# Another order for the front of a two-layer trunk: attention scores before v and u, modulation chunks under routing and residuals, ring slots by release

## The chip, the cores and the metric

The kernel runs on one core of one Trainium2 chip. The metric is device time in microseconds of one execution. Before the change three runs gave a median of 911.49 us (908.78 to 912.89).

## What is computed

`x` is 256 tokens by 1,024 channels, `c` one vector of 1,024; everything is float32. There are two layers. The reference, cut to what matters here:

```
cs = silu(c)
for i in range(2):
    sh_m, sc_m, g_m, sh_f, sc_f, g_f = split(cs @ w_mod[i] + b_mod[i], 6)     # 6 vectors of 1024
    h = rmsnorm(x) * (1 + sc_m) + sh_m
    y = hybrid_ab(h) if i == 0 else multiscale_pool(h)
    x = x + g_m * y
    h = rmsnorm(x) * (1 + sc_f) + sh_f
    x = x + g_f * hier_moe(h)      # 32 experts, 2 per token, chosen in 1 of 4 groups
hybrid_ab: q, kv_lat, q_idx, k_idx, w_idx, u, v = split(h @ w_in)
    A: indexer score picks 64 keys per query (top_k); 8 heads of 64 share one k, v
       made from rmsnorm(kv_lat) @ w_kv_up; softmax with a distance penalty; p @ v
    B: gelu(u) * (W_s @ layernorm(gelu(v)) + b_s), per chunk of 128 positions
    concat(A, B) @ w_o
```

## The kernel before

Each engine has a program of its own with its order written out by hand; semaphores (`S[...]`) join them. Nothing is reordered at run time, so on each engine a waiting instruction holds all that is queued behind it. TensorE's program is `_(pe)`, ScalarE's `_(act)`, VectorE's `_(dve)`, GpSimd's `_(pool)`; the loads of the large weights are issued by SyncE (`_(sp)`).

**The ring.** The tile `ring` has four slots of 2 MB. `plan` lists 31 chunks in the order in which TensorE uses them: 24 chunks `("mod", m)` (a modulation vector has two, m = 0 to 11 for layer 0 and 12 to 23 for layer 1), qi, kv, q, v and u of `w_in`, and two halves of `w_o`. Chunk n goes to slot n % 4 and is loaded once chunk n - 4 has been used (`chunk_done`). After the 21st chunk the expert loop of layer 0 takes over the ring: a pair of experts needs two slots for gate and up (4 MB) and the tile `dn_w` for down (2 MB); the last pair's down goes into the ring too. After that loop ten more chunks come, then the expert loop of layer 1. `FIRST` is the index of the first chunk after the first loop, `pair_slots` the two slots of a pair.

**Modulation.** `mod_chunk(m)` multiplies a chunk into four partial sums in a PSUM bank (line 424, 16 instructions); ScalarE copies them out (line 775, `mod_split`); `finish(m)` then sums them: a gate by two kinds of row matmul (lines 432 and 433), which ScalarE keeps in `gates` (line 779), or, after the second half of a shift or scale, a column of 8 values per partition by one-column matmuls (line 442, and 445 where the bias comes from `rows`; those are the "natural" ones of layer 1's mixer). The order is set by `mod_run(ms)`, on TensorE one chunk ahead of the finish, on ScalarE copy and keep chunk by chunk. `scale_shift` on VectorE waits for the columns (`col_kept`), and `modulated` makes `hT`, which all projections read.

**Layer 0's front.** On TensorE: mods 0 to 3, qi, kv, mods 4 and 5, indexer scores (`head_units`, line 522), `w_s` turned, q (line 482), v (543), mods 6 and 7, k and v of the attention (549, 551), u (482), mods 8 and 9, the spatial gating (563), attention scores (522), then turns of p (579) and p @ v (587), the output projection (610). VectorE selects the 64 keys meanwhile (lines 1096 to 1098), then does gelu and layernorm of v, gelu of u, `shift(u)` (penalty, mask, maximum; from line 1135) and `divide(u)` for six units of heads.

**Residual and routing.** `residual` adds the gated branch in four parts; ScalarE's `squares` and VectorE's `normed` follow, `turn` transposes (470). `route(l)`: router logits (624), the choice on VectorE with small count matmuls between (630 to 640), the selection matrix `sel` (1250), gathering of tokens (648), four rows turned (653). Then `experts(l)`: per pair gate and up (672), turn (682), down (694), combine (708). In `route(0)` TensorE runs mods 10 and 11 ahead of `turn` and mods 22 and 23 behind line 653; ScalarE has `squares` behind `mod_run(10, 11)`. Behind `experts(0)` come mods 12 to 15, `turn(2)`, mods 16 and 17, pooling (749), and in `route(1)` mods 18 to 21.

Of the kernel before, what the change touches and what calls it, by code (L numbers as in the profile page):

```python
# [37 lines left out]
def trunk(nc, x, c, w_mod, b_mod, norm_mix, norm_ffn, w_in, kv_norm, w_kv_up, sgu_norm, w_s, b_s, w_o,  # L38
# [19 lines left out]
    with ExitStack() as ctx:  # L58
# [48 lines left out]
        def chunk_at(n):  # L107
            s = (n % CH) * KT * HALF
            return ring[:, s:s + KT * HALF].rearrange("p (k n) -> p k n", k=KT)

# [13 lines left out]
        qiT, gtmp, qT, uT = ar(0, 1024, t=4), ar(1024, 1024, t=2), ar(2048, 1024, t=4), ar(3072, 1024, t=4)  # L124
# [6 lines left out]
        ws_raw, usq = ar(3072, 512, g=4), ar(0, 1024, t=4)  # L131
# [3 lines left out]
        att1 = hT[:, :, :].rearrange("p k t -> p (k t)").rearrange("p (h s) -> p h s", h=8)  # L135
# [19 lines left out]
        def v3(a, n):  # L155
# [15 lines left out]
        chunk_dmas = [2 if key == ("in", "kv") else 1 for key in plan]  # L171

        def arrivals(n):
            return 16 * sum(chunk_dmas[i] for i in range(n % CH, n + 1, CH))

        def mod_part(m):
            return dn_w[:, 1, 0, :] if 12 <= m < 22 else gates[:, 3, :]
# [17 lines left out]
            mix_done sgu_done bT_ready  # L195
# [15 lines left out]
        def pair_slots(l, b):  # L211

            first, second = ((FIRST, len(plan))[l] + 2 * b) % CH, ((FIRST, len(plan))[l] + 2 * b + 1) % CH
            return min(first, second), max(first, second)
# [12 lines left out]
        def _(sp):  # L227
# [5 lines left out]
            def chunk(n):  # L233

                kind, what = plan[n]
                dst, arrived = chunk_at(n), chunk_in[n % CH]
# [33 lines left out]
            for l in range(L):  # L270
# [3 lines left out]
                if l == 1:  # L274
                    sp.wait_ge(S["mix_done"], 10)
                    sp.wait_ge(S["col_kept"], len(columns))
# [16 lines left out]
                if l == 0:  # L293

                    first, second = pair_slots(l, 0)
# [104 lines left out]
        def _(pe):  # L400
            def arrived(key):

                n = chunk_no[key]
                pe.wait_ge(chunk_in[n % CH], arrivals(n))
# [6 lines left out]
            def mod_chunk(m):  # L411
# [8 lines left out]
                if m == 11:  # L420
                    pe.wait_ge(S["pT_ready"], 6)
# [79 lines left out]
            pe.wait_ge(S["small_in"], 16 * SMALL)  # L501
# [95 lines left out]
            for v in range(2, 6):  # L597
                turn_p(v)
# [810 lines left out]
```

## Time and profile before

| what | value |
|---|---|
| median of 3 runs | 911.49 us |
| the profiled execution | 918.24 us, span 916.5 us |
| TensorE busy, its weight loads | 780.9 us (85%), 387.7 us (42%) |
| VectorE, ScalarE, GpSimd busy | 241.9, 162.7, 36.8 us |
| moved | 269.59 MB, 294 GB/s over the span |
| mean granted TensorE clock | 0.891 of full |

### The profile page before, as it was taken

Reading aid. Unit: us, or ns where it says so; the run is one execution under the profiler, and the core shown is the slowest. Engines: PE = TensorE matmul, PEld = TensorE weight load, DVE = VectorE, ACT = ScalarE, POOL = GpSimd, SP = SyncE. Lnnn points to the kernel's source line nnn. Section 1 sums busy time; section 2 is a strip of 40 time slices with the busy share of each in tenths; the row PEclk is TensorE's granted clock in tenths of the full one; section 3 lists DMA queues with packets and bytes.
Section 4 is the critical chain, followed back from the end, with each engine's and each line's share of the span. In section 5 each row is a group of like instructions: output and inputs, shape, how many; then the busy total and the mean of one; then the engine's idle time right before and its main releaser. Section 6 shows DMA issues by size and latency. Waiting matters only on the chain.

```text
span 916.5 us, 9000 instructions
## 1 busy us (share of the span) xinstructions
PE 780.9 (85%) x3194; PEld 387.7 (42%) x3194; DVE 241.9 (26%) x667; ACT 162.7 (18%) x331; POOL 36.8 (4%) x63
## 2 busy tenths in 40 slices
PE   3689999689567989999999969965898999999994
PEld 1375767343462333333333327454533333333331
DVE  0013621811251221212122222524322121212123
ACT  2013021410212211212121102021212111212111
POOL 7200000000200000000000000002000000000000
PEclk9687998589568999999999987865899999999998
DMA  9949267105605999999999799556099999999961
GB/s 308 329 146 351 83 236 257 68 0 188 270 1 195 374 421 421 397 423 414 423 414 421 311 340 346 185 189 270 1 356 422 420 408 418 408 419 407 419 261 46
DMA packets 62138, 269.59 MB, mean 294 GB/s; under 512 B 3950, under 2 KB 6094, under 8 KB 37536
## 3 DMA queue, kind: packets, MB, share of 16 engines
q1 hardware_dynamic: 61152, 268.22, 74.3%
q0 software_dynamic: 960, 1.02, 0.5%
q8 instruction: 16, 0.26, 0.1%
q14 instruction: 10, 0.08, 0.0%
HBM read 268.18 MB, written 1.05 MB: 294 GB/s over the span
## 4 chain that ended last, share of the span: by engine, by line
PE 40%; issue 32%; DMA 18%; DVE 4%; ACT 3%; SPq 1%; POOL 1%; ACTq 0%; DVEq 0%; POOLq 0%
DMA ring<-in_w_up 13%; PE bank L672 7%; PE bank L482 5%; DMA ring<-in_w_mod 5%; PE bank L424 4%; PE bank L694 3%; PE bank L442 3%; PE bank L610 3%; PE bank L543 1%; PE bank L433 1%; PE bank L522 1%; PE bank L470 1%; PE bank L432 1%; PE bank L587 1%; PE bank L648 1%
## 5 line engine op out<-in xcount | busy, mean ns | idle before, releaser
L672 PE MATMUL bank<-ring,arena 128*64 128x512 f32 x1024 | 230.4, 602 | 31.4 <-DMA ring<-in_w_up 26.4
L672 PEld LDWEIGHTS bank<-ring,arena 128*64 128x64 f32 x1024 | 82.9, 138 | 158.6 <-issue 151.9
L708 PE MATMUL bank<-arena 128*128 128x512 f32 x256 | 117.9, 604 | 0.0
L694 PE MATMUL bank<-dn_w,hT 128*64 128x512 f32 x480 | 108.8, 592 | 0.6 <-DMA dn_w<-in_w_down 0.6
L1292 DVE SCALAR_TENSOR_TENSOR hT<-hT,bank 128x256 f32<-128x256 f32 x32 | 13.5, 421 | 238.0 <-ACT hT L935 238.0
L708 PEld LDWEIGHTS bank<-arena 128*128 128x128 f32 x256 | 46.2, 189 | 71.2 <-issue 71.2
L424 PE MATMUL bank<-ring,cs 128*32 128x512 f32 x384 | 53.6, 698 | 19.0 <-DMA ring<-in_w_mod 18.3
L694 PEld LDWEIGHTS bank<-dn_w,hT 128*64 128x64 f32 x480 | 40.0, 137 | 63.8 <-issue 61.8
L482 PE MATMUL bank<-hT,ring 128*128 128x256 f32 x192 | 47.4, 413 | 2.9 <-ACT hT L803 2.9
L935 ACT ACTIVATE hT<-bank 128x256 f32<-128x256 f32 x32 | 12.3, 383 | 190.8 <-PE bank L672 190.8
L928 ACT COPY arena<-arena 128x512 f32 x68 | 42.3, 622 | 16.7 <-issue 14.4
L482 PEld LDWEIGHTS bank<-hT,ring 128*128 128x128 f32 x192 | 40.2, 211 | 9.3 <-ACT hT L803 3.0
L1315 DVE COPY arena<-bank 128x512 f32<-128x512 f32 x32 | 22.1, 691 | 66.3 <-PE bank L694 66.3
L948 ACT COPY arena<-bank 128x512 f32<-128x512 f32 x32 | 18.7, 585 | 102.1 <-PE bank L694 102.1
L424 PEld LDWEIGHTS bank<-ring,cs 128*32 128x32 f32 x384 | 12.1, 121 | 51.0 <-issue 28.7
L337 POOL TENSOR_TENSOR stat<-stat,mhalf 128x2 f32<-128x2 f32 x5 | 3.5, 696 | 736.5 <-DVE stat L999 736.5
L470 PE MATMUL bank<-ident,xn 128*128 128x128 f32 x64 | 14.7, 423 | 16.5 <-DVE xn L1003 16.5
L941 ACT COPY hT<-bank 128x256 f32<-128x256 f32 x32 | 11.9, 373 | 93.0 <-PE bank L682 93.0
L610 PE MATMUL bank<-ring,xn 128*128 128x512 f32 x64 | 27.7, 593 | 0.8 <-issue 0.8
L648 PE MATMUL bank<-sel,xn_parts 128*128 128x512 f32 x64 | 19.4, 470 | 9.8 <-DVE sel L1250 9.8
L1303 DVE COPY hT<-arena 128x1 f32 (+1 forms) x32 | 4.9, 153 | 83.8 <-PE bank L708 83.8
L648 PEld LDWEIGHTS bank<-sel,xn_parts 128*128 128x128 f32 x64 | 17.3, 331 | 11.5 <-DVE sel L1250 10.1
(254 smaller groups left out, 660.3 us busy)
## 6 DMA issues: line engine op xcount, KB each, us to landing
ring<-in_w_gate SPq DMA_DIRECT2D x32, 2048.0 KB, 12.9
ring<-in_w_up SPq DMA_DIRECT2D x32, 2048.0 KB, 17.3
dn_w<-in_w_down SPq DMA_DIRECT2D x30, 2048.0 KB, 9.5
ring<-in_w_mod SPq DMA_DIRECT2D x24, 2048.0 KB, 14.5
ring<-in_w_in SPq DMA_DIRECT2D x4, 2048.0 KB, 9.2
ring<-in_w_o SPq DMA_DIRECT2D x2, 2048.0 KB, 12.9
ring<-in_w_down SPq DMA_DIRECT2D x2, 2048.0 KB, 13.9
x_res<-in_x SPq DMA_DIRECT2D x2, 512.0 KB, 4.3
```

The lines of the kernel that those rows point to most:

```text
L424: ins = pe.matmul(bank[m % 2][q:q + 32, :], cs[:, 2, k:k + 1].to_broadcast([P, 32]), w[:, k, :], start=(k < 4), stop=(k >= 4))
L442: ins = pe.matmul(bank[1][:, k:k + 1], src, pick4[:, 0:1], start=True, stop=not natural)
L470: ins = pe.transpose(bank[2 + kk][:, a:a + P], turned(xn, t, k, natural), ident[:])
L482: ins = pe.matmul(bank[banks[m // 2]][:, (m % 2) * T:(m % 2 + 1) * T], w[:, k, m * P:(m + 1) * P], hT[:, k, :], start=(k == 0), stop=(k == ...
L610: ins = pe.matmul(bank[(3, 4, 6, 7)[2 * half + t]][:, :], catT[:, k, t * P:(t + 1) * P], w[:, k, :], start=(k == 0), stop=(k == KT - 1))
L648: ins = pe.matmul(bank[2 + k % 4][:, :], turned(xn_parts[:, part], t, k, False), sel[:, t, :], start=(t == 0 and part == 0), stop=(t == TT ...
L672: ins = pe.matmul(bank[2][h * WIN:(h + 1) * WIN, :], xw[:, b, h, k, :], w[:, h, :, k, :], start=(k == 0), stop=(k == KT - 1))
L694: ins = pe.matmul(bank[n][h * WIN:(h + 1) * WIN, :], actT[:, t, h * WIN:(h + 1) * WIN], w[:, h, t, n * HALF:(n + 1) * HALF], start=(t == 0 ...
L708: ins = pe.matmul(bank[4 + 2 * n + t][:, :], ct[:, b, t * P:(t + 1) * P], y_s[:, b, n * HALF:(n + 1) * HALF], start=(isinstance(p, int) an ...
L928: ins = act.copy(xw[:, b, h], xgT[:, :, bass.ds(start, WIN)])
L948: act.copy(y_s[:, b, 0:HALF], bank[0][:, :]).then_inc(e["y_act"], 1)
L1315: dve.tensor_copy(y_s[:, b, HALF:D], bank[1][:, :]).then_inc(e["y_dve"], 1)
```

## The change

- **Plan.** Chunks 6 to 9 leave the attention for the stretch behind the output projection; 12 and 13 move from behind the first expert loop to the routing of layer 0; 22 and 23 from there to the routing of layer 1. Fourteen mod chunks before the first loop and ten behind it, as before.
- **Ring slots.** `slot_of(n)` gives the chunks behind the first loop the slots 1, 3, 0, 2, the order in which the loop lets them go. Only the fourth of them waits for the loop's last down matmul, and the pooling weights are issued behind the fourth instead of behind the second. `pair_slots` for layer 1 gives slots 0, 2 and 1, 3 in place of 3, 0 and 1, 2.
- **Scratch.** `gtmp`, `usq` and the second half of the scores (`att1`) lie in `dn_w` in place of `arena` and `hT`, so `hT` lives on for v and u. Partial sums of shifts and scales always go to `gates[:, 3]`, so the SyncE queue no longer waits for `col_kept` ahead of layer 1's first down weights.
- **Order of the front.** TensorE: the gates of mods 4 and 5 finish behind the indexer scores; q, k and v, attention units 0 to 2, first half of v, units 3 to 5, second half, turns 0 and 1, p @ v of the first tokens, first half of u, turns 2 and 3, spatial gating, second half of u, turns 4 and 5, the rest. VectorE: all shifts and divides, then gelu and layernorm of v, the gating, gelu of u last.
- **Order of route and residual.** ScalarE's `mod_run` is split into `part`, `keep_gate` and `keep_column`, put one by one among the other work; `squares` comes behind two copies.

The diff, cut to its core:

```diff
-                ("mod", 6), ("mod", 7), ("in", "u"), ("mod", 8), ("mod", 9), ("out", 0), ("out", 1)]
-        plan += [("mod", m) for m in (10, 11, 22, 23, *range(12, 22))]
+                ("in", "u"), ("out", 0), ("out", 1)]
+        plan += [("mod", m) for m in (6, 7, 8, 9, 12, 13, 10, 11, *range(14, 24))]
-        FIRST = plan.index(("mod", 12))
+        FIRST = plan.index(("mod", 14))
+        def slot_of(n):
+            return n % CH if n < FIRST else (1, 3, 0, 2)[(n - FIRST) % CH]
         # SyncE, chunks behind the first expert loop
-                        elif n % CH == second:
+                        elif slot_of(n) == pair_slots(l, 0)[1]:
                             sp.wait_ge(E[l]["down_done"], groups * 2)
                         else:
-                            sp.wait_ge(E[l]["unit_done"], groups * 2 - (n % CH == first))
+                            sp.wait_ge(E[l]["unit_done"], groups * 2 - (slot_of(n) == pair_slots(l, 0)[0]))
                         chunk(n)
-                        if n == FIRST + 1:
-                            sp.wait_ge(E[l]["down_done"], groups * 2 - 1)
+                        if n == FIRST + CH - 1:
         # TensorE, front (behind the indexer scores)
+            finish(4)
+            finish(5)
             by_channel(("in", "q"), (5, 7), S["q_done"])
...
+            att = qT, kT, (6, 7, 2), S["att_done"], S["att_shift"]
+            head_units(range(0, 3), *att)
+            project_v(0)
+            head_units(range(3, 6), *att)
+            project_v(1)
+            turn_p(0)
+            turn_p(1)
+            pe.wait_ge(S["v_kept"], 2)
+            pe.wait_ge(S["pT_ready"], 2)
+            values(0)
+            project_u(0)
+            turn_p(2)
+            turn_p(3)
...
+            project_u(1)
+            turn_p(4)
+            turn_p(5)
+            pe.wait_ge(S["sgu_kept"], 1)
             pe.wait_ge(S["pT_ready"], 6)
             values(1)
         # TensorE, route(l)
-                mod_run((range(10, 12), range(18, 21))[l])
+                a = (6, 18)[l]
+                mod_chunk(a)
+                mod_chunk(a + 1)
+                finish(a + 1)
+                mod_chunk(a + 2)
+                mod_chunk(a + 3)
                 turn(2 * l + 1)
+                finish(a + 3)
...
                 ins.then_inc(S["lg_done"], 1)
+                a = (12, 22)[l]
+                mod_chunk(a)
+                mod_chunk(a + 1)
                 pe.wait_ge(S["asg_ready"], l + 1)
...
+                if l == 0:
+                    finish(13)
+                    mod_chunk(10)
+                    mod_chunk(11)
+                else:
+                    finish(22)
+                    finish(23)
                 pe.wait_ge(S["sel_ready"], l + 1)
...
                 if l == 0:
-                    mod_run(range(22, 24))
+                    finish(10)
+                    finish(11)
         # TensorE, behind experts(0)
-            mod_run(range(12, 16))
+            mod_chunk(14)
+            mod_chunk(15)
+            finish(15)
             turn(2, natural=True)
-            mod_run(range(16, 18))
+            mod_chunk(16)
+            mod_chunk(17)
+            finish(16)
+            finish(17)
         # ScalarE, behind experts(0); route(l) is likewise part, part, squares, keep_column, part, part, ...
-            mod_run(range(12, 14))
+            part(14)
             squares(2)
-            mod_run(range(14, 16))
+            part(15), keep_column(15)
         # VectorE, front
+            shift(0), shift(1), shift(2), divide(0), divide(1), shift(3), shift(4), shift(5), divide(2), divide(3), divide(4), divide(5)
+            gelu_v()
+            keep_heads(0)
             dve.wait_ge(S["sgu_done"], 1)
...
+            dve.wait_ge(S["u_kept"], 2)
+            gelu_poly(flat(usq), flat(uT), S["u_poly"])
+            dve.wait_ge(S["u_tanh"], 1)
+            stt(flat(uT), flat(usq), 1.0, flat(uT), ALU.add, ALU.mult).then_inc(S["u_ready"], 1)
             stt(catT[:, 4:8, :], catT[:, 4:8, :], 0.5, uT, ALU.mult, ALU.mult).then_inc(S["bT_ready"], 1)
-            shift(2), divide(1), shift(3), divide(2), shift(4), keep_heads(0), divide(3), shift(5), divide(4), divide(5)
             keep_heads(1)
```

## Rows read from the trace of the kernel before

**Rows 1.** Windows by stage: busy time of each engine, granted clock, DMA share and rate.
```profile
core 0: us, PE busy (x) PEld busy (x) DVE busy (x) ACT busy (x) POOL busy (x), PEclk, DMA share, GB/s
92.20:193.40 101.20, 89.62 (x347) 60.78 (x346) 43.90 (x155) 22.59 (x59) 0.69 (x1) 0.80 0.41 146
...
221.20:286.30 65.10, 42.73 (x192) 28.14 (x190) 22.75 (x92) 15.96 (x28) 5.35 (x3) 0.69 0.44 171
286.30:533.90 247.60, 232.11 (x932) 89.98 (x934) 53.09 (x116) 41.12 (x80) 0.00 (x0) 0.99 0.95 386
533.90:654.60 120.70, 89.39 (x429) 61.33 (x429) 46.51 (x139) 22.85 (x44) 6.06 (x4) 0.72 0.63 237
```

**Rows 2.** Timeline of TensorE, 107 to 221 us: start, length, line, tiles.
```profile
107.77 13.90 PE L543 MATMUL bank<-ring,hT 128*128 128x512 f32 x32
121.60 3.64 PE L424 MATMUL bank<-ring,cs 128*32 128x512 f32 x32
125.94 3.96 PE L442 MATMUL bank<-pick,gates 128*128 128x1 f32 x16 [0.70 <-ACT gates L775]
...
171.08 2.07 PE L522 MATMUL bank<-arena 64*128 64x256 f32 x4 [4.68 <-DVE amax L1141]
...
186.70 5.91 PE L587 MATMUL bank<-arena 128*128 128x512 f32 x8 [0.67 <-ACT arena L887]
193.44 27.70 PE L610 MATMUL bank<-ring,xn 128*128 128x512 f32 x64 [0.83 <-issue]
```

**Rows 3.** Timeline of VectorE and ScalarE, 148 to 232 us.
```profile
148.24 1.23 DVE L1088 TENSOR_TENSOR arena<-arena 128x1024 f32<-128x1024 f32 x1
...
221.98 0.69 DVE L1035 TENSOR_TENSOR x_res<-x_res,hT 128x512 f32<-128x512 f32 x1
...
231.89 1.06 ACT L795 ACTIVATE xn<-x_res 128x1024 f32<-128x1024 f32 x1
```

**Rows 4.** Timeline of TensorE, 241 to 295 us.
```profile
241.57 7.01 PE L624 MATMUL bank<-wroute,hT 128*128 128x36 f32 x32 [1.26 <-issue]
253.83 0.64 PE L630 MATMUL bank<-rt,before 128*128 128x32 f32 x2 [5.25 <-DVE rt L1218]
...
263.15 9.43 PE L648 MATMUL bank<-sel,xn_parts 128*128 128x512 f32 x32 [4.92 <-DVE sel L1250]
...
274.30 3.64 PE L424 MATMUL bank<-ring,cs 128*32 128x512 f32 x32
...
286.31 8.98 PE L672 MATMUL bank<-ring,arena 128*64 128x512 f32 x32 [2.92 <-ACT arena L928]
```

**Rows 5.** SyncE's queue: the issues at both ends of the first expert loop.
```profile
295.48 0.40 SPq L259 DMA_DIRECT2D ring<-in_w_gate  x1
...
504.66 22.77 SPq L240 DMA_DIRECT2D ring<-in_w_mod  x2
```

**Rows 6.** Timeline of TensorE, 526 to 627 us.
```profile
526.80 7.13 PE L708 MATMUL bank<-arena 128*128 128x512 f32 x16
...
545.91 3.64 PE L424 MATMUL bank<-ring,cs 128*32 128x512 f32 x16 [6.44 <-DMA ring<-in_w_mod]
...
554.95 0.58 PE L445 MATMUL bank<-ident,rows 9*128 9x1 f32 x2
...
570.03 3.64 PE L424 MATMUL bank<-ring,cs 128*32 128x512 f32 x32
...
576.94 2.07 PE L432 MATMUL bank<-rows,row_sel 9*128 9x512 f32 x2 [1.16 <-ACT dn_w L775]
...
619.21 7.02 PE L624 MATMUL bank<-wroute,hT 128*128 128x36 f32 x32 [2.84 <-ACT hT L803]
```

**Rows 7.** Timeline of VectorE and ScalarE at the two residuals behind the loop.
```profile
536.48 0.69 DVE L1035 TENSOR_TENSOR x_res<-x_res,hT 128x512 f32<-128x512 f32 x1
...
555.63 1.06 ACT L795 ACTIVATE xn<-x_res 128x1024 f32<-128x1024 f32 x1
...
598.46 1.06 ACT L795 ACTIVATE xn<-x_res 128x1024 f32<-128x1024 f32 x1 [4.73 <-DVE x_res L1035]
```

More of the change, by code:

```diff
@@ L211, in pair_slots @@
         def pair_slots(l, b):
[L213 to L214 removed]
+            n = (FIRST, len(plan))[l] - CH + 2 * b
+            return min(slot_of(n), slot_of(n + 1)), max(slot_of(n), slot_of(n + 1))
         def of_pair(view, l, b):
@@ L509, in _, with head_units @@
             ins.then_inc(S["kt_turned"], 1)
-            def head_units(lhs, rhs, banks, done, consumed):
-                for u in range(6):
+            def head_units(units, lhs, rhs, banks, done, consumed):
+                for u in units:
                     t, per = (0, 4) if u < 2 else (1, 2)
@@ L538, in _ @@
             by_channel(("in", "q"), (5, 7), S["q_done"])
-            pe.wait_ge(S["score_relu"], 5)
-            w = arrived(("in", "v"))
-            for t in range(TT):
-                for k in range(KT):
-                    ins = pe.matmul(bank[3 + t][:, :], hT[:, k, t * P:(t + 1) * P], w[:, k, :],
-                                    start=(k == 0), stop=(k == KT - 1))
-                ins.then_inc(S["v_done"] if t == 0 else S["chunk_done"], 1)
-            mod_run(range(6, 8))
             pe.wait_ge(S["gain_ready"], 1)
@@ L609, in _ @@
                     for k in range(KT):
+                        if half == 0 and t == 0 and k == 4:
+                            pe.wait_ge(S["bT_ready"], 1)
                         ins = pe.matmul(bank[(3, 4, 6, 7)[2 * half + t]][:, :], catT[:, k, t * P:(t + 1) * P], w[:, k, :],
@@ L768, in _, with part, keep_gate, keep_column @@
         def _(act):
[L769 to L786 removed]
+            def part(m):
+                act.wait_ge(S["chunk_done"], chunk_no["mod", m] + 1)
+                act.copy(mod_part(m)[:, (m % 2) * HALF:(m % 2 + 1) * HALF], bank[m % 2][:, :]).then_inc(S["mod_split"], 1)
+                if mods[m // 2] not in GATE:
+                    act.wait_ge(S["mod_split"], turn_of[m] + 1)
+                    act.sem_inc(S["mod_kept"], 1)
+            def keep_gate(m):
+                act.wait_ge(S["gate_done"], 1 + [x for x in turn_of if mods[x // 2] in GATE].index(m))
+                act.copy(gates[:, GATE[mods[m // 2]], (m % 2) * HALF:(m % 2 + 1) * HALF], bank[m % 2][:, :]).then_inc(S["mod_kept"], 1)
+            def keep_column(m):
+                v = columns.index(mods[m // 2])
+                act.wait_ge(S["col_done"], v + 1)
+                act.copy(raw_col[:, v, :], bank[1][:, 0:KT]).then_inc(S["col_kept"], 1)
             def squares(n):
@@ L841, in _, with keep_v @@
                 act.copy(flat(qT[:, 2 * i:2 * i + 2, :]), bank[b][:, :]).then_inc(S["q_kept"], 1)
-            for t in range(TT):
+            act.wait_ge(S["kup_done"], 1)
+            act.copy(arena[:, 11008:11520], bank[2][:, :]).then_inc(S["kup_kept"], 1)
+            def keep_v(t):
                 if t == 0:
@@ L848, in _, with keep_u @@
                 act.activation(gtmp[:, t, :], bank[3 + t][:, :], ACT.Square).then_inc(S["v_kept"], 1)
-            mod_run(range(6, 8))
-            act.wait_ge(S["kup_done"], 1)
-            act.copy(arena[:, 11008:11520], bank[2][:, :]).then_inc(S["kup_kept"], 1)
-            act.wait_ge(S["v_poly"], 1)
-            act.activation(flat(gtmp), flat(gtmp), ACT.Tanh, scale=GELU_C).then_inc(S["v_tanh"], 1)
-            act.wait_ge(S["ws_turned"], 1)
-            act.wait_ge(S["score_done"], 6)
-            for i, b in enumerate((6, 5)):
+            def keep_u(i):
                 if i == 0:
```

196 lines of the change are left out of this document (95 added, 101 removed).

## The prediction

> **What bounds the kernel now.** I read the windows by stage first. The reader is to see four kinds of stretch. The expert loops run at 386 GB/s and more over their windows and TensorE's clock is at its upper level [rows 1]; from the slot release at 295.5 us to the load of the last slots at 504.7 us [rows 5] transfers set the pace, so a loop of this length stays as it is and only its start moves. The start is the moment at which TensorE has used the first pair (the gate and up loads at 295.48 follow the matmuls of 286.31, length 8.98) [rows 4, 5]. The other three stretches, attention (101.2 us), routing of layer 0 (65.1 us) and the passage between the loops (120.7 us), move 146 to 237 GB/s, and no engine fills them: TensorE is busy for 89.6, 42.7 and 89.4 us at clocks of 0.80, 0.69 and 0.72 [rows 1]. There the order of TensorE's program sets the time, with waits for VectorE and ScalarE in it. All that the change moves lies in these three.
>
> Then I read the timeline of TensorE through each of them [rows 2, 4, 6] and the timelines of the other two engines where TensorE waits [rows 3, 7]. Two places stand out. Behind the first loop x is written at 536.48 + 0.69 = 537.2 us, and its squares begin on ScalarE at 555.63 [rows 7]: 18.4 us in which they stood behind copies and a column of modulation chunks whose data came late (the third chunk's matmuls start at 545.91 after 6.44 us of waiting for a transfer) [rows 6]. After the output projection it is the same on a smaller scale: x at 222.7, squares at 231.89 [rows 3].
>
> **Term 1, attention.** Four chunks leave (two runs of 3.64), two columns (3.96 each) and two waits of 0.70 [rows 2]: 7.3 + 7.9 + 1.4 = 16.6 us. The stretch had 101.2 - 89.6 = 11.6 us of idle TensorE [rows 1], 10.2 without those two waits, the longest 4.68 us for VectorE's shift [rows 2]. In the new order the shifts, exponentials and divides of six units lie beside 13.9 us of v [rows 2], so most of this goes. New waits come: about 1.2 us until k and v are copied, about 1.5 until v is copied and p turned, and at the end gelu of u, which is now last. That tail is ScalarE's eviction of the second half, a short and a long pass of the polynomial, the tanh, two products and the copy of the heads: seven steps at no more than 1.23 us [rows 3], 8 us with their hand-overs. Two turns and p @ v (5.91) [rows 2] run beside it, so some 1 us is bare. TensorE then needs 89.6 - 15.2 = 74.4 us and about 4 of waits: 78.4, or 22.8 less. The gates of mods 4 and 5 move out of the way of the scores and come back behind them; I count 1 us for their two waits. Denser work should also keep the clock up, where p @ v took 5.91 for eight instructions of 512 columns and the output projection 27.70 for 64 [rows 2], which is 0.74 against 0.43 each; I take 1 us. Sum: -25. Bounds: if all 10.2 us of idle time stay, -17.6; if the bare waits vanish and the clock stays up, -29. The block is nearer to the second, since the work that TensorE waited for has 13.9 us of v beside it.
>
> **Term 2, to the router logits.** Before, the projection's end at 221.1 to the logits at 241.57: 20.4 us [rows 2, 4]. After: mods 6 and 7 (3.6), ScalarE's copy (0.6), a column (4.0), mods 8 and 9 (3.6, or 5.4 if the first falls to the lower clock, as at 545.91, where 16 instructions took 3.64 against 32 in 3.64 at 570.03 [rows 6]), the turn (3.6, an estimate: the same 16 transposes take no more than the chunk pair beside them), a column (4.0), 2.8 until hT is there: 22.2 to 24.0, so +1.8 to +3.6; I take +2.5. Squares and norm are hidden under the column and mods 8 and 9. SyncE can load mod 9 only when the projection ends; it is wanted 12 us later, and a chunk of 2.1 MB at the loop's rate is 5.4 us of transfer [rows 1].
>
> **Term 3, routing of layer 0.** From the logits to the offsets it takes 263.15 - 4.92 - 241.57 = 16.7 us [rows 4]. Mods 12 and 13 fall into the 5.25 us gap [rows 4] and last 3.6 at the upper level or 5.4 with the first low: free. Behind the offsets TensorE had 4.92 us to wait for `sel` [rows 4]. Now a column of the natural kind stands there, and mods 10 and 11. That column took from 549.55 (where the chunk ends) to 555.5, 6.0 us [rows 6], its last instructions 0.58 each; all of it at that pace is about 8.2. With 5.4 for the chunks that is 13.6 against 4.9: +8.7; at the upper clock 6.0 + 3.6, so +4.7. The chunks bring the clock up before the gathering, worth 1.5 of its 9.43. Then the biggest change here: after line 653's rows, mods 22 and 23 with two gates stood in front of the first window, 286.31 - 274.30 = 12.0 us [rows 4]. Now only two gates (4.2) stand there, beside ScalarE's window copies: 5 us, -7. The first pair may take 7.1 in place of 8.98 [rows 4]: -1.9. Sum 8.7 - 1.5 - 7 - 1.9 = -1.7; bounds -6 and +2. Front in all: -25 + 2.5 - 1.7 = -24.2, carried whole through the first loop. Its second pair's weights are issued after mod 11, some 19 us before they are wanted.
>
> A rule of the Trainium skill (TensorE: Matmul & The Clock Gate, What's actually happening) says that the throttled state is the default and activity releases it. The trace agrees where it can be seen (16 instructions in 3.64 us behind a wait of 6.44 [rows 6]). By the rule I would charge both chunks of each of the four pairs that stand behind a stretch of light work (8 and 9, 12 and 13, 10 and 11, 20 and 21) at the lower level: 866 where my sum gives 859.
>
> **Term 4, behind the first loop** (in the times of before). Squares no longer queue behind two copies, a column and a third chunk. Mods 14 and 15 end at 533.9 + 3.8 = 537.7 if they are there; squares run from 537.2 to 539.4, the second copy ends at 540.0, the natural column (6.05) at 546.1, `turn(2)` (3.6) at 549.7, where before TensorE stood there at 570.03 [rows 6]: -20.3. Are the chunks there? One is loaded at 504.66 in both kernels; the other issue of that row had to wait for the loop's last down matmul, its 22.77 us [rows 5]. In the new slot order the second and third wait only for the last gate and up, about 515.4, 11.5 us sooner. With the last two downs they make 10.5 MB from 504.7 on, 27 us at 386 GB/s [rows 1], so the lot is in by 532. Mods 17, 18 and 19 and the pooling weights follow at 527 to 538 and are wanted at 550 to 570; mods 20 and 21 at about 552 and 554, wanted at 575. Hidden, with 10 us or more of cover.
>
> **Term 5, pooling and the second residual.** From 570.03 to the squares at 598.46: 28.4 us [rows 6, 7]. It keeps VectorE's pooling and TensorE's matmuls; the gate of mod 17 no longer waits 1.16 us and should not fall to 2.07 a pair [rows 6]: -2.9.
>
> **Term 6, to the logits of layer 1.** Before 619.21 - 598.46 = 20.8 us [rows 6, 7]. After: mods 18 and 19 and the first column run beside the residual; then mod 20 (3.6), mod 21 (1.8), turn (3.6), column (4.0), 2.8: 15.9 counted from x, so -4.9. Routing of layer 1 takes mods 22 and 23 (5.4) into its gap of 5.2 and two gates (4.1) under the 4.9 of `sel`: 0, with the cover that rows 4 show for layer 0. Passage in all: -20.3 - 2.9 - 4.9 = -28.1. Bounds: -18, if transfers keep 10 us of it, and -31.
>
> The wait for `col_kept` on SyncE goes too, at nothing: the column came before the logits at 619.21, and the load behind it is first used by the loop, which begins where the window ends, at 654.60 [rows 1, 6]. Slots of a pair 0 and 2, 1 and 3: at nothing, as pairs one and three slots apart alternate in the first loop of before, which keeps 386 GB/s over both [rows 1].
>
> **Sum.** -24.2 - 28.1 = -52.3. The profiled execution took 918.24; 865.9 after. It stands 6.75 above the median of the runs, so against 911.5 I predict 859 us.
>
> **Rivals.**
> (a) The block becomes VectorE's. It is busy for 43.9 of 101.2 us [rows 1], and gelu of u is now its last work. If the idle time stays, term 1 is -17.6: 866.5. Against it: its share is under a half.
> (b) The late chunks stay bound by transfers: ten chunks and the pooling weights are 22 MB in a passage that moved 237 GB/s [rows 1], and a chunk waited for one for 6.44 us [rows 6]. Term 4 loses 10: 869.
> (c) The lower clock holds through both chunks of a pair, not only the first, as the 3.64 us for 16 instructions behind a wait [rows 6] would allow: 1.8 us on each of four pairs (8 and 9, 12 and 13, 10 and 11, 20 and 21), 7.2: 866.5. This is what the rule quoted above comes to.
> (d) Attention runs without waits and at the upper level, term 3 at its good bound: 4 + 4.3 less, 851.
> (e) Slower: the loops' rate falls, by the new distance of a pair's slots in layer 1. It decides from 52 / 14 = 3.7 us on each pair's 15 us. A fall of 4 us per pair would give 915. Nothing in the rate of before (distance one and three alike) speaks for it.
> That the change does nothing would need the 18.4 us of [rows 7] to come back elsewhere; no other engine is near its limit there.
>
> **Chances.** The sum as it stands, 853 to 864: 0.53. (a) 0.12, (b) 0.10, (c) 0.10, (d) 0.13, (e) 0.02. The range over them, 848 to 876, leaves out (e), and parts of (a) and (b) that come together. A measurement of this kernel tells about 0.5% (4.6 us) from no change. Faster by more than that: 0.97; within it: 0.01; slower: 0.02.
>
> **What would show it.** The output projection starts near 168 us, not 193; logits of layer 0 near 219; the first pair near 264 with the first slot release near 271. Squares behind the first loop begin within 2 us of x. From the loop's end to the first pair of layer 1 it takes 93 us, not 121. The loops keep 14.9 us a pair (504.66 - 295.48 over 14 pairs [rows 5]). The prediction is wrong if TensorE waits for VectorE before the projection for over 5 us, if chunks behind the loop wait for transfers, or if the gathering starts more than 10 us after `sel`.

## The result and the profile after

Four runs of the changed kernel gave a median of 842.60 us (841.06 to 850.91), against 911.72 us (908.78 to 912.89) for the kernel before: a ratio of 0.923 (95% interval 0.918 to 0.928). The profiled execution took 841.06 us, its span 839.3 us, the mean granted clock 0.935. The direction was right and the size was not: 859 was forecast, with 848 to 876 around it, and the gain of the medians is 69 us instead of 52.

The windows by stage of the changed kernel, with the same borders by work as in [rows 1]: attention from q to the output projection, routing of layer 0, first expert loop, passage, second loop.

```profile
core 0: us, PE busy (x) PEld busy (x) DVE busy (x) ACT busy (x) POOL busy (x), PEclk, DMA share, GB/s
...
89.80:153.20 63.40, 58.27 (x252) 41.87 (x250) 38.87 (x133) 20.41 (x54) 0.69 (x1) 0.98 0.29 100
...
180.80:244.90 64.10, 60.12 (x313) 40.07 (x312) 22.82 (x92) 17.21 (x31) 5.33 (x3) 0.79 0.86 328
244.90:490.30 245.40, 231.91 (x933) 89.73 (x932) 52.96 (x116) 41.84 (x81) 0.00 (x0) 0.99 0.97 395
490.30:580.20 89.90, 81.17 (x405) 53.36 (x404) 46.24 (x139) 23.83 (x44) 6.04 (x4) 0.81 0.78 289
580.20:839.30 259.10, 233.99 (x932) 90.67 (x932) 59.44 (x126) 43.48 (x84) 0.69 (x1) 0.97 0.86 352
```

The reader is to see the first and the fourth row. Attention went from 101.2 to 63.4 us and its clock from 0.80 to 0.98; TensorE's busy time fell by 31.4 us, though only 15.2 us of work left. The passage went from 120.7 to 89.9 us. Routing takes 64.1 us against 65.1, but with eight chunks in it where there were four, and the loops are within 3 us of before.

The timeline of TensorE in the attention block and behind it:

```profile
106.69 2.21 PE L522 MATMUL bank<-arena 64*128 64x128 f32 x20 [0.77 <-ACT arena L887]
108.83 7.13 PE L558 MATMUL bank<-ring,hT 128*128 128x512 f32 x16
115.89 2.00 PE L522 MATMUL bank<-arena 64*128 64x256 f32 x12
117.83 7.13 PE L558 MATMUL bank<-ring,hT 128*128 128x512 f32 x16
124.80 1.04 PE L582 MATMUL bank<-ident,arena 128*128 128x128 f32 x8
127.19 1.95 PE L590 MATMUL bank<-arena 128*128 128x512 f32 x4 [1.36 <-ACT arena L922]
...
147.86 3.67 PE L590 MATMUL bank<-arena 128*128 128x512 f32 x8 [1.36 <-ACT arena L925]
153.17 27.70 PE L631 MATMUL bank<-ring,xn 128*128 128x512 f32 x64 [1.63 <-issue]
...
203.99 7.02 PE L649 MATMUL bank<-wroute,hT 128*128 128x36 f32 x32 [2.84 <-ACT hT L846]
210.94 5.74 PE L425 MATMUL bank<-ring,cs 128*32 128x512 f32 x32
...
225.62 5.23 PE L425 MATMUL bank<-ring,cs 128*32 128x512 f32 x32
230.78 8.20 PE L683 MATMUL bank<-sel,xn_parts 128*128 128x512 f32 x32
...
244.91 7.09 PE L708 MATMUL bank<-ring,arena 128*64 128x512 f32 x32
```

The wait of 4.68 us for VectorE [rows 2] is gone, and p @ v of the last tokens takes 3.67 us for the same eight instructions that took 5.91 [rows 2]. The output projection begins at 153.2 instead of 193.4.

### The profile page after: what moved, and what is told of

The parts are those of the page before. It is cut to its first block, busy times and chain, and to the rows that moved or that the text cites. A ratio compares the mean times of both kernels' runs of the same rounds, so it can differ in the third digit from the quotient of the medians.

```text
span 839.3 us, 9002 instructions
## 1 busy us (share of the span) xinstructions
PE 755.8 (90%) x3194; PEld 369.7 (44%) x3194; DVE 241.5 (29%) x667; ACT 163.1 (19%) x331; POOL 36.8 (4%) x63
## 4 chain that ended last, share of the span: by engine, by line
PE 41%; issue 34%; DMA 18%; ACT 2%; DVE 2%; SPq 1%; POOL 1%; DVEq 0%; POOLq 0%; ACTq 0%
DMA ring<-in_w_up 14%; PE bank L708 8%; PE bank L425 5%; PE bank L483 4%; PE bank L733 4%; PE bank L443 4%; PE bank L631 3%; DMA ring<-in_w_mod 3%; PE bank L558 2%; PE bank L568 2%; PE bank L747 1%; PE bank L683 1%; PE bank L471 1%; PE bank L434 1%; PE bank L433 1%
## 5 line engine op out<-in xcount | busy, mean ns | idle before, releaser
L708 PE MATMUL bank<-ring,arena 128*64 128x512 f32 x1024 | 230.2, 602 | 23.2 <-DMA ring<-in_w_up 21.4
L425 PE MATMUL bank<-ring,cs 128*32 128x512 f32 x384 | 58.9, 764 | 11.1 <-DMA ring<-in_w_mod 10.7
L1370 DVE COPY arena<-bank 128x512 f32<-128x512 f32 x32 | 22.1, 691 | 66.4 <-PE bank L733 66.4
L443 PE MATMUL bank<-pick,gates 128*128 128x1 f32 x128 | 31.1, 358 | 4.6 <-ACT gates L815 4.6
L815 ACT COPY gates<-bank 128x512 f32<-128x512 f32 x24 | 14.0, 585 | 108.5 <-PE bank L425 108.5
L483 PE MATMUL bank<-hT,ring 128*128 128x256 f32 x128 | 32.0, 417 | 2.9 <-ACT hT L846 2.9
L443 PEld LDWEIGHTS bank<-pick,gates 128*128 128x128 f32 x128 | 29.5, 311 | 10.5 <-ACT gates L815 8.6
L483 PEld LDWEIGHTS bank<-hT,ring 128*128 128x128 f32 x128 | 27.2, 214 | 8.3 <-ACT hT L846 3.0
## 6 DMA issues: line engine op xcount, KB each, us to landing
ring<-in_w_up SPq DMA_DIRECT2D x32, 2048.0 KB, 17.2
```

Source lines behind the costliest of these rows:

```text
L425: ins = pe.matmul(bank[m % 2][q:q + 32, :], cs[:, 2, k:k + 1].to_broadcast([P, 32]), w[:, k, :], start=(k < 4), stop=(k >= 4))
L443: ins = pe.matmul(bank[1][:, k:k + 1], src, pick4[:, 0:1], start=True, stop=not natural)
L483: ins = pe.matmul(bank[banks[m // 2]][:, (m % 2) * T:(m % 2 + 1) * T], w[:, k, m * P:(m + 1) * P], hT[:, k, :], start=(k == 0), stop=(k == ...
L708: ins = pe.matmul(bank[2][h * WIN:(h + 1) * WIN, :], xw[:, b, h, k, :], w[:, h, :, k, :], start=(k == 0), stop=(k == KT - 1))
L1370: dve.tensor_copy(y_s[:, b, HALF:D], bank[1][:, :]).then_inc(e["y_dve"], 1)
```

## The experiments

Every kernel was timed beside the kernel before. One more thing is needed for reading them: the changed kernel itself, run again with six runs beside the last experiments, gave 846.41 us (841.90 to 852.03), ratio 0.9257 (0.9209 to 0.9306). Medians 4 us apart are therefore not told apart here, and the small effects below are read from windows.

> The changed kernel itself, on the chip of the three others, for comparison: 843 us within 3 us by every theory.

The passage of that run was 494.73 to 584.80, 90.1 us, against 90.0 in the first profile; its attention block 90.30 to 154.28, 64.0 against 63.4. Over all kernels below that leave a stretch as it is, the attention block lasts 62.9 to 64.2 us (eight executions) and the passage 89.5 to 92.0 (six executions). A difference of 2 us in the block means something, one of 2 us in the passage does not. The first expert loop, whose program is the same in all of them, lasts from the first pair to its last combine 245.4 to 248.9 us, the second 257.8 to 263.4; of the 5.9 us between the two executions of the changed kernel 4.9 lie in the two loops.

**1. The attention order alone undone.**

```diff
+            w = arrived(("in", "v"))
+            for t in range(TT):
+                for k in range(KT):
+                    ins = pe.matmul(bank[3 + t][:, :], hT[:, k, t * P:(t + 1) * P], w[:, k, :],
+                                    start=(k == 0), stop=(k == KT - 1))
+            by_channel(("in", "u"), (6, 5), S["u_done"])
...
+            head_units(range(6), qT, kT, (6, 7, 2), S["att_done"], S["att_shift"])
...
-            head_units(range(0, 3), *att)
-            project_v(0)
-            head_units(range(3, 6), *att)
-            project_v(1)
...
-            project_u(0)
-            turn_p(2)
-            turn_p(3)
+            for v in range(2, 6):
+                turn_p(v)
...
-            project_u(1)
-            turn_p(4)
-            turn_p(5)
```

The gating stands between u and the units again, as before; ScalarE and VectorE have their old order with it.

> The changed kernel with the attention block (from q to the output projection) in the order of the kernel before, everything else as changed. Three theories of why the block lost 40 us and not 25. Clock: the light work (score units, turns, values, gating) fell to 1.2 GHz because it stood together behind waits; then the block keeps that here: TensorE's clock over it 0.75 to 0.85, 18 to 24 us longer than in the changed kernel, about 863 us. Moves: the chunks and one-column matmuls that left the block had lowered the clock; then it stays above 0.93 here and the block is only 8 to 11 us longer (the waits), about 852 us. Waits alone: clock unchanged at 0.80 but no more than 12 us longer, about 853 us.

Measured: 859.98 us (857.53 to 865.04), ratio 0.942 (0.936 to 0.948). The block and its last part:

```profile
91.00:169.74 78.74, 67.30 (x252) 45.79 (x250) 38.29 (x130) 20.60 (x54) 0.69 (x1) 0.84 0.23 81
134.00:169.74 35.74, 24.30 (x85) 13.94 (x83) 22.57 (x86) 14.00 (x43) 0.00 (x0) 0.67 0.17 59
```

It holds the same 252 matmul instructions as the changed kernel's block, but they are busy for 67.3 us instead of 58.3, and idle time is 11.4 us instead of 5.1. So the order is worth 15.3 us: 9.0 by the clock and 6.3 by waits. (By the medians it is 17.4 us, or 13.6 against the 846.41 of the changed kernel run again.) The waits theory falls; of the two others the first comes nearest (clock 0.84 where it said 0.75 to 0.85, block 15 us longer where it said 18 to 24), with a part left to the second, as the kernel before had 0.80.

**2. The columns put back.** To that kernel two runs of eight one-column matmuls are added, about where modulation's columns stood (the first now comes behind k and v of the attention instead of ahead of them). The chunks that stood ahead of the columns are not put back.

```diff
+            for k in range(KT):     # ahead of u, and again behind it
+                pe.matmul(bank[0][:, k:k + 1], slot_no[:, :].rearrange("p (q k) -> p k q", k=4)[:, k % 4], ones[:, 0:1], start=True, stop=True)
```

> The kernel with the old attention order again (block 78.7 us, clock 0.84), with two runs of eight one-column matmuls on constants, result unused, ahead of and behind u, where the columns of modulation stood before the change. If light columns pull the clock down for what follows: the block grows by the 8 us of the columns and 4 to 7 us more, u's first instructions and the gating at the lower level, about 871 us. If they only take their own time: 8 us, 868 us, and the gating keeps its 1.95 us.

Measured: 872.83 us (870.87 to 873.80), ratio 0.954 (0.949 to 0.960), 12.9 us above the median of the kernel without them. Timeline and window:

```profile
118.98 3.79 PE L559 MATMUL bank<-ones,slot_no 128*128 128x1 f32 x16
122.63 15.74 PE L483 MATMUL bank<-hT,ring 128*128 128x256 f32 x64
138.21 3.68 PE L564 MATMUL bank<-ones,slot_no 128*128 128x1 f32 x16
141.76 2.53 PE L570 MATMUL bank<-arena 128*128 128x128 f32 x16
144.22 8.25 PE L522 MATMUL bank<-arena 64*128 64x128 f32 x28
```
```profile
89.23:179.51 90.28, 80.07 (x283) 57.22 (x282) 39.09 (x133) 20.60 (x54) 0.69 (x1) 0.80 0.20 71
```

The block grew by 11.5 us, of which the two runs are 7.5. TensorE's busy time grew by 12.8 us (80.07 against 67.30), so its neighbours took 5.3 us more, and 1.2 us of idle time went. The neighbours ran at the lower level in part or in whole: u took 15.74 us (granted clock 0.89) where it took 13.98 without the columns (1.00), the gating 2.53 (0.77) where it took 1.95 (1.00), the six score units 10.3 where they took 7.8, and the clock of the block is back at the 0.80 of [rows 1]. The columns cost more than their own time.

**3. Dense work that nobody needs, in the waits.**

```diff
+                pe.matmul(bank[0][:, :], ones[:], slot_no[:], start=True, stop=True)   # 2, 2, 4 ahead of units 3, 4, 5; 1 ahead of each of turns 2 to 5
```

> The kernel with the old attention order again, with twelve matmuls of 512 columns on constants into an unused bank (work that nobody needs, 0.86 us each at the upper level, 10 us in all) put in front of TensorE's waits there: two, two and four before units 3, 4 and 5, one before each of turns 2 to 5. Clock theory: the granted clock over the last 36 us of the block rises from 0.67 above 0.9, the light instructions behind take half the time, and the block ends 2 to 6 us sooner in spite of the added work: about 856 us where it was 860. Waits theory: the added work shows, 2 us or more slower: 862 us or more.

Measured: 859.68 us (854.51 to 863.06), ratio 0.942 (0.937 to 0.947).

```profile
136.74 1.99 PE L514 MATMUL bank<-slot_no,ones 128*128 128x512 f32 x4
138.66 1.13 PE L529 MATMUL bank<-arena 64*128 64x256 f32 x4
...
146.69 1.13 PE L529 MATMUL bank<-arena 64*128 64x256 f32 x4 [0.31 <-DVE amax L1179]
147.75 1.09 PE L589 MATMUL bank<-ident,arena 128*128 128x128 f32 x8
```
```profile
134.00:164.33 30.33, 25.85 (x99) 13.04 (x98) 22.55 (x86) 12.98 (x41) 0.00 (x0) 1.00 0.20 69
```

The clock is 1.00 where it was 0.67, score units take 1.13 us where they took 2.07 and eight transposes (two turns) 1.09 where they took 1.97, and in this execution the block is 74.8 us instead of 78.7 with about 10 us of work added. That the light instructions were slow by the clock and not by their operands is shown. As a time the two kernels are the same: the medians are 0.3 us apart and not the 4 that I had expected. The profiled execution of this kernel was its fastest and that of experiment 1 its slowest, so the 3.9 us of the profiles are no measure of the gain, and it is no recipe.

**4. Scores first, but v and u whole.**

```diff
-            head_units(range(0, 3), *att)
+            head_units(range(6), *att)
             project_v(0)
-            head_units(range(3, 6), *att)
             project_v(1)
...
-            project_u(0)
-            turn_p(2)
-            turn_p(3)
+            for v in range(2, 6):
+                turn_p(v)
...
+            project_u(0)
             project_u(1)
-            turn_p(4)
-            turn_p(5)
```

ScalarE's copies of v and of u move behind the exponentials and the copies of p with it.

> The changed kernel with all six score units ahead of v and u, but v and u whole instead of in halves between the light work. Clock theory: turns, values and gating stand together again, the granted clock over the block falls below 0.9 and light instructions double in time; with 6 to 8 us of waits the block is 10 to 16 us longer, about 856 us. Waits theory: 6 to 8 us longer and the clock stays above 0.95, about 850 us. If the halves do nothing: 843 us.

Measured: 858.93 us (857.41 to 859.20), ratio 0.941 (0.936 to 0.947).

```profile
90.67:169.51 78.84, 65.83 (x252) 46.37 (x250) 37.71 (x128) 20.50 (x54) 0.69 (x1) 0.89 0.23 80
```

As slow as the old order: idle 13.0 us (7.9 more than in the changed kernel) and busy time 7.6 us more for the same instructions. Computing the scores early brings nothing by itself. It is the four dense halves of 7.1 us between the light pieces that do both things, cover the waits and hold the clock (in the changed kernel each half ran at a granted clock of 1.00).

**5. The passage: slots, squares, both.**

```diff
-            return n % CH if n < FIRST else (1, 3, 0, 2)[(n - FIRST) % CH]
+            return n % CH
```
```diff
-            part(14)
-            squares(2)
-            part(15), keep_column(15)
+            part(14), part(15), keep_column(15)
+            squares(2)
```

With the old slots `pair_slots` and the place where the pooling weights are issued go back too.

> The changed kernel with the old ring slots behind the first loop (n % 4; the second chunk behind the loop waits for the last down matmul again). Slots theory: the second modulation chunk lands some 5 to 8 us after it is wanted and the passage grows by that, about 849 us. Queue theory (only the place of the squares counts): no change, 843 us.

> The changed kernel with the squares of the second residual behind both copies and the column again. Queue theory: norm and turn then begin only after the column, 6 to 9 us later, about 851 us. Slots theory (the early chunks gave the gain): within 2 us of the changed kernel, 844 us.

> The changed kernel with both the old ring slots and the late squares (each alone cost 2 to 3 us). If they lie on one chain behind one another: passage 3 to 5 us longer, about 847 us. If each covers for the other: 8 us or more, 851 us and up.

Measured: old slots 844.88 us (840.90 to 846.98), ratio 0.925 (0.919 to 0.931); late squares 845.82 (843.72 to 846.13), 0.927 (0.921 to 0.932); both 846.15 (845.12 to 847.01), 0.927 (0.922 to 0.931). None of the three is told apart from the changed kernel by its time. Their passages:

```profile
490.82:582.85 92.03, 83.73 (x406) 54.70 (x405) 46.31 (x139) 23.85 (x44) 6.04 (x4) 0.78 0.83 311
```
```profile
492.21:583.10 90.89, 78.91 (x406) 51.50 (x405) 46.22 (x139) 23.84 (x44) 6.04 (x4) 0.81 0.76 282
```
```profile
491.55:584.69 93.14, 79.74 (x406) 52.25 (x405) 46.20 (x139) 23.84 (x44) 6.03 (x4) 0.82 0.82 307
```

That is 2.0, 0.9 and 3.1 us more than 90.0. The first two lie within the 89.5 to 92.0 of passages left as in the changed kernel, so neither effect is told from nothing (experiment 1, with the new slots, has 92.0 as well); the third is 1.1 us above them. The rows say why so little is left, first with the old slots, then with late squares:

```profile
493.85 1.92 PE L425 MATMUL bank<-ring,cs 128*32 128x512 f32 x16 [1.10 <-DMA ring<-in_w_mod]
...
506.74 3.67 PE L471 MATMUL bank<-ident,xn 128*128 128x128 f32 x16 [4.84 <-DVE xn L1053]
```

With the old slots the second chunk's wait for its transfer is only 1.10 us; I had expected 5 to 8. With late squares the turn starts 14.5 us after the loop's last combine instead of 12.9: it needs the norm and the column, and with early squares the column ends last, 13.0 us after the loop, with late ones the norm, 14.5 us after it. Both expectations of some 8 us were wrong.

**6. Chunks 12 and 13 back in the passage.**

```diff
-        plan += [("mod", m) for m in (6, 7, 8, 9, 12, 13, 10, 11, *range(14, 24))]
+        plan += [("mod", m) for m in (6, 7, 8, 9, 22, 23, 10, 11, *range(12, 22))]
...
+            mod_chunk(12)
+            mod_chunk(13)
+            finish(13)
             mod_chunk(14)
```

Chunks 22 and 23 go back into the routing of layer 0, so the passage holds ten chunks here as in the changed kernel and in the one before. The scratch lies in `dn_w` again, and SyncE waits for `col_kept`.

> The changed kernel with chunks 12 and 13 back behind the first loop and 22 and 23 back in the routing of layer 0 (in the places that 12 and 13 held), the scratch of partial sums in the down tile again. Moved-out theory: the passage gets back two chunks (3.6 us), a column of 6 us and waits for transfers, 12 to 16 us; the routing of layer 0 loses the column of 6 us but has two gates of 4 in its place; about 854 us. Order theory (slots and squares gave the gain): within 3 us of the changed kernel.

Measured: 856.66 us (854.59 to 857.78), ratio 0.937 (0.933 to 0.942).

```profile
490.07:594.37 104.30, 84.92 (x429) 59.75 (x429) 46.28 (x139) 23.02 (x43) 6.04 (x4) 0.75 0.67 249
```

14.3 us more in the passage, as the moved-out theory said, while routing of layer 0 took 40.2 us from logits to first pair, against 40.9 with the other pair in it. Where the pair 12 and 13 stands is the largest single piece of the passage. The number of chunks in it is the same; it is the place that counts. Behind the loop the pair and its column stand ahead of the turn, which starts 25.2 us after the loop instead of 12.9. Chunks 22 and 23, which the changed kernel has in the passage in their stead, lie in the routing of layer 1, where TensorE otherwise waits 5.23 and 4.92 us for VectorE, and cost less than nothing: from logits to first pair it takes 33.6 us with them and 35.6 here without them, since the eight small count matmuls behind them run at the upper level (0.39 us for two instructions instead of 0.61) and are done 1.7 us sooner.

**7. All three undone.**

```diff
     # the edits of 5 and 6 together; TensorE: mods 12, 13, 14, column of 13, mod 15, column of 15
-            part(12)
-            squares(2)
+            part(12), part(13), keep_column(13)
+            squares(2)
```

> The changed kernel with all three parts of the passage undone at once: chunks 12 and 13 back in it (alone 14.3 us of the passage), the old ring slots (alone 2.0) and the late squares (alone 0.9). If the three cover for one another: the passage, 90.0 us in the changed kernel, becomes 112 to 120 us (120.7 before) and the time about 867 us or more. If they only add up: 107 us and about 860 us.

Measured: 866.56 us (861.88 to 871.08), ratio 0.947 (0.941 to 0.953). Timeline and window of the passage:

```profile
506.91 3.64 PE L426 MATMUL bank<-ring,cs 128*32 128x512 f32 x16 [6.29 <-DMA ring<-in_w_mod]
```
```profile
495.37:607.47 112.10, 87.17 (x429) 59.89 (x429) 46.27 (x139) 22.94 (x43) 6.04 (x4) 0.74 0.68 255
```

The wait of 6.3 us for the third chunk [rows 6] is back. Alone the three cost 14.3 + 2.0 + 0.9 = 17.2 us, together 22.1. Slots and squares cost 7.8 us where the pair stands in the passage (112.1 against 104.3) and 3.1 where it does not. Part of the reason is in the rows: here the third chunk lands 11.5 us after the loop and TensorE wants it at 5.2, while without the pair it wants its third chunk only at 17.1 (experiment 5, old slots). 8.6 us are left to the 120.7 of [rows 1]. They lie between mods 16 and 17, behind the turn, and the logits of layer 1 (40.6 us here, 49.2 before), where this kernel keeps the new order; no run divides them further.

**8. Dense work ahead of the router logits.**

```diff
+                heat(2)      # pe.matmul(bank[7][:, :], ones[:], slot_no[:], start=True, stop=True), twice
                 hT_ready(2 * l + 2)
```

> The changed kernel with two such matmuls in the 2.8 us wait ahead of the router logits in each layer. If dense work there brings the clock up: the logits (7.0 us at 0.5) take about 3.6 to 5 us, 2 to 3 us a layer, about 838 us. If the clock does not rise in time: the two take 3.6 us at the lower level, 1 us more than the wait in each layer, about 845 us.

Measured: 846.71 us (845.01 to 850.31), ratio 0.927 (0.922 to 0.933), not told apart from the changed kernel.

```profile
200.31:203.87 3.56, 3.56 (x6) 1.44 (x6) 2.40 (x7) 2.75 (x6) 0.00 (x0) 0.50 1.05 387
203.87:210.68 6.81, 6.81 (x34) 6.74 (x32) 0.00 (x0) 1.23 (x2) 4.66 (x2) 0.50 1.02 376
```

Behind a column of 3.9 us the two matmuls ran at 0.50 in layer 0, and the clock did not rise for the logits either. In layer 1, behind the same turn and column, it did:

```profile
547.85 3.60 PE L638 MATMUL bank<-slot_no,ones 128*128 128x512 f32 x4
551.29 3.88 PE L655 MATMUL bank<-wroute,hT 128*128 128x36 f32 x32
```

There the logits ran at 0.92 and took 3.88 us instead of 7.01. Yet the first pair of layer 1 started 36.8 us after the column's end, against 36.7 in the changed kernel, so the 3 us were lost again on the way to it. I had expected one answer for both layers; there were two, and the time shows no gain.

**9. A faster version.**

```diff
-                    if natural:
-                        ins = pe.matmul(bank[1][:, k:k + 1], rows[:, k * P:(k + 1) * P], ident[0:9, r:r + 1], start=False, stop=True)
+                # the bias of the two natural columns: GpSimd loads nat_bias, scale_shift adds it on VectorE
+                    done(tt(ab[:, l, which + 1, :], s, nat_bias[:, 0, :], ALU.add))
+                    done(stt(ab[:, l, which, :], a, 1.0, nat_bias[:, 1, :], ALU.add, ALU.add))
...
+            keep_heads(1)
             stt(catT[:, 4:8, :], catT[:, 4:8, :], 0.5, uT, ALU.mult, ALU.mult).then_inc(S["bT_ready"], 1)
-            keep_heads(1)
```

> A faster version of the changed kernel, if the theory of the routing and the passage holds, that TensorE's own program is what counts there: the natural columns of chunks 13 and 15 lose their eight bias matmuls each (the bias comes by a transfer and is added on VectorE), 3 us each off the path, and VectorE copies the heads ahead of the product with u, 1 us: 7 us less than the changed kernel, about 836 us. If something else bounds these stretches: no more than 2 us.

Measured: 832.15 us (831.10 to 836.95), ratio 0.911 (0.907 to 0.916), against 0.926 for the changed kernel on the same chip: faster than both kernels, by 14 us of the medians.

```profile
154.17 27.70 PE L632 MATMUL bank<-ring,xn 128*128 128x512 f32 x64 [0.93 <-issue]
...
186.15 3.96 PE L447 MATMUL bank<-pick,gates 128*128 128x1 f32 x16 [0.71 <-ACT gates L816]
...
218.54 1.95 PE L447 MATMUL bank<-pick,gates 128*128 128x1 f32 x16
```
```profile
181.81:239.77 57.96, 53.73 (x298) 35.46 (x297) 22.84 (x92) 17.21 (x31) 5.36 (x3) 0.82 0.90 343
487.44:572.64 85.20, 76.94 (x389) 49.62 (x389) 46.29 (x139) 23.83 (x44) 6.05 (x4) 0.82 0.81 304
```

I had expected 7 us, so the gain is twice that. The routing window lost 6.1 us and the passage 4.8. In the routing the natural column went from 6.4 us to 1.95: half of its matmuls are gone, and the clock, which fell in the middle of it in the changed kernel, was at 0.96. In the passage it went from 6.9 to 3.57, at 0.50. The early copy of the heads took 0.7 us off the wait ahead of the projection (1.63 to 0.93). These make 11.6 us; the other 2 to 3 us lie within the spread of the changed kernel's runs.

## Why the prediction was right or wrong

Against its own execution the sum was -52.3 us and the span shrank by 77.2. That is more than the medians' 69 us because the profiled execution of before stood 6.5 us above the median of 911.72 and the one of after 1.5 below its own. Term by term, in spans:

| term | forecast | measured |
|---|---|---|
| 1, attention, to the projection's start | -25 | 153.17 - 193.44 = -40.3 |
| 2, projection's end to logits | +2.5 | 23.2 against 20.5: +2.7 |
| 3, logits to the end of the first pair | -1.7 | 48.0 against 53.7: -5.7 |
| first loop behind it | 0 | -0.3 |
| 4 to 6, passage | -28.1 | 90.0 against 120.7: -30.7 |
| second loop | 0 | 259.1 against 261.9: -2.8 |

**The step that failed is term 1, and in it the sentence "denser work should also keep the clock up; I take 1 us".** The work that leaves (16.6 us) was right and the waits were nearly right: 11.6 us of idle time became 5.1, with "about 4" forecast. From q's start the block lost 37.8 us: 16.6 moved, 5.1 of waits, and 16.1 by the clock. Experiments 1 and 2 divide the last: 9.0 us belong to the new order, against the same instructions in the old one, and 7.1 to what had gone besides, chunks and columns. Of the 7.1 the two columns' effect on their neighbours is 5.3; the other 1.8 stay open, and each figure is from one execution. The other 2.4 us of the 40.3 lie ahead of q, where the forecast had 1 us for the gates; q starts between 89.2 and 94.1 us in the executions with this front, so nothing is read from them.

The rows had it. A clock of 0.80 over 101.2 us [rows 1] says that two fifths of the block, 40 us, were at the lower level. Rows 2 held 0.74 us for an instruction of p @ v and 0.43 for one of the projection. The 0.74 is not even the price of the lower level, as the granted clock over it (186.70 to 192.60) was 0.62; [rows 6] held the full ratio of two, 16 instructions of a chunk in 3.64 us against 32 in 3.64. I read the two figures and priced the clock at 1 us without multiplying it out over the units, turns, gating and p @ v.

The bound of -29 was wrong for the same reason: it allowed the waits to vanish and the clock the same 1 us. Rival (d), which had attention without waits and at the upper level, took its price from that bound, so the range ended at 848, above three of the four runs. (d) is what happened in kind (clock 0.98, though 5.1 us of waits stayed), at 16 us for the clock and not 1. None of the three signs of being wrong that I had named came: they asked for waits, and not for a price that was too low.

**Terms 2 and 3.** Term 2 came as forecast; mods 8 and 9 took 6.45 us, more than the 3.6 to 5.4, and the turn 2.04 instead of 3.6, both by the clock. In term 3 the natural column (6.4) and the chunks (5.23) were +6.7 and not +8.7, the offsets were done 1.3 us sooner, as chunks ahead of the count matmuls had brought the clock up (0.39 us for two instructions instead of 0.61), which the forecast had at nothing, and the first pair began right behind the gates: 40.9 us from logits to pair instead of 44.7, and 7.09 instead of 8.98 for the pair. Rival (c), both chunks of each pair at the lower level, did not come true: 6.45, 5.74, 5.23 and 5.34 us for the four pairs, where one chunk at 1.2 GHz makes 5.5 and both 7.3. Each pair began at the lower level (granted clock 0.50 to 0.53 over its first 1.4 us) and ended above it. By the rule of the Trainium skill (TensorE: Matmul & The Clock Gate, What's actually happening) that the throttled state is the default and activity releases it, the trace agrees for the start of each pair.

**Terms 4 to 6.** Their sum was right within 3 us, and the turn behind the loop ended 16.5 us after the combine, 19.6 sooner than before, for a forecast of 20.3. But the story was partly another. I gave the early squares and the ring slots as the reason; experiments 5 and 6 show that, each undone alone, they hold 1 to 2 us, no more than unchanged passages differ by, and that the place of chunks 12 and 13 holds 14.3. With that pair still in its old place slots and squares hold 7.8 (experiment 7). The sum came out right because it compared the two orders in full, in which the pair no longer stands ahead of the turn. For routing of layer 1 the forecast was 0 and it became 1.8 us shorter (33.6 against 35.4), by the count matmuls as above. Rival (b) fell: no TensorE wait for a transfer stands in the passage of after. Of the second loop's 2.8 us 1.7 are the first pair at the upper level (7.09 against 8.78); the rest is less than that loop differs by from one execution to the next.

Rivals (a) and (e) fell: VectorE is busy for 38.9 of 63.4 us with TensorE waiting 5.1, and the loops kept their pace. From the third load of gates to the first chunk behind the loop it was 461.53 - 252.20 = 209.3 us, where [rows 5] have 209.2, with the distance of slots as before; in layer 1 the new distance shows no cost, as the loop there is not slower.

## What to carry to other kernels

Before you cost a stretch of small matmuls, read its granted clock and multiply: (1 - clock) times twice its length is the time at the lower level, and half of the busy part of that is the most that the upper level would give back. Here that is 40 us and at most 20, and 16 came; dense work between the light pieces gave 9 of them. Leave out instructions that take the same time at both levels, as the stepped columns below. Work moved out of a stretch is worth its own time plus what it did to the clock of its neighbours; one-column matmuls cost here half as much again as they last. A chunk pair is free, or better, in a gap where TensorE waits anyway, and dear ahead of something that all wait for. When several edits meet on one chain, undo each alone and all together before you name the one that paid: here the squares, which looked like the cause, held 1 us alone, slots and squares 3 together and 8 with the pair in its old place, and the place of the pair 14. And time the stretch in kernels that leave it alone before you read 2 us out of it.

## What the hardware showed unexpectedly

The time of a one-column matmul depended on how its stationary operand lies. A column of 16 instructions whose operand is read in steps lasts 3.96 us at a granted clock of 0.98 ([rows 2], its first), and 3.96 us in experiment 9 as well, where the clock was 0.94. With the operand read in order, as the two natural columns have it, the same count took 1.95 us in experiment 9, at 0.96, and 3.57 us in that run's passage (493.56 to 497.13) at 0.50. The stepped one took 3.96 us at 0.50 too (601.17 to 605.13 in the kernel before). So the ordered column follows the clock, while the stepped one takes the same time at both levels, which is twice the ordered one's at the upper level.
